# A hybrid decoder step: eight expert steps per block of the second group instead of twelve, and value rows one unit behind the key rows

## Chip, cores and metric

One Trainium2 chip, one core of it. The time is the device time of one execution in microseconds (us). Compared are medians of several executions.

## What is computed

The kernel takes 544 tokens of 2048 channels: a prompt of 512, and 8 samples of 4. They pass a recurrent branch and a convolution branch, which are merged by gates, and then an expert mixer. All parameters are shared. The part that the change touches is the mixer:

```python
q = (xb @ w_q).astype(f32).reshape(PEER_BLOCK, PEER_HEADS, 2, D_HALF)
s1 = jnp.einsum('thd,hkd->thk', q[:, :, 0], keys1.astype(f32))
s2 = jnp.einsum('thd,hkd->thk', q[:, :, 1], keys2.astype(f32))
v1, i1 = lax.top_k(s1, PEER_TOPK)
v2, i2 = lax.top_k(s2, PEER_TOPK)
...
e = (jnp.take_along_axis(i1, si // PEER_TOPK, axis=-1) * N_KEYS
     + jnp.take_along_axis(i2, si % PEER_TOPK, axis=-1))
g = jax.nn.softmax(sv, axis=-1)
u = u_tab[e]
act = jax.nn.gelu(jnp.einsum('thkd,td->thk', u, xb).astype(f32))
v = v_tab[e]
return jnp.einsum('thk,thkd->td', (g * act).astype(xb.dtype), v)
```

Each token has 8 heads, and each head picks 16 of 16384 experts. For each pick a key row of `u_tab` and a value row of `v_tab` (8 KB each) are read.

## The kernel before

Tokens stand in tiles of 128 partitions. A *unit* is one head of one tile, or for the sample tile one of two packed units: there are 34. One *row* of a unit is one pick for 128 tokens: a gather of 1.05 MB by an indirect DMA, issued by POOL. A key row is multiplied with the normalised tokens and summed on VectorE (a dot). A value row is scaled by the pick's weight and added.

The tokens are treated in two groups. Group 0 (the last prompt tile and the samples) goes through branches, w_out and w_q first. It has the first 10 units, 160 rows of either kind. Group 1 (three prompt tiles, 384 columns) follows, with 24 units. While PE multiplies for group 1, VectorE works on the rows of group 0. This is written out by hand in *expert steps*: step p does the dot of key row p (`dot_row`, L1174) and adds value row p - 18 (`value_row`, L1183). There are 178 steps; from step 160 on they hold value rows alone. At row 1 of a unit the weights of the unit before are made (`expert_weights`, L1169), and at row 3 the next unit is routed (`route`, L1131 to L1164: sorting, indices, gates). The functions `steps_branch`, `steps_out` and `steps_query` say which steps stand in which block:

- the branch stage has eight blocks; in each PE makes four products (192 matmul records, 12 weight pieces of 0.5 MB) and VectorE merges two rows of them (`merge`, L1071 to L1075). On VectorE a block holds four steps, the merges of the block before, and eight more steps;
- w_out has sixteen output rows in eight products of 64 records, each with two steps and an addition (`add_rows`, L1098), which waits for a transpose on PE (L1477);
- w_q has eight heads with four steps each. Its scores are copied by ScalarE (`head`). ScalarE follows the same table: the activation of a unit's dots (L827) and the exponents of the next (L822) stand behind the head of that place;
- what is left of the 178 steps comes behind w_q.

POOL issues the gathers in one order, key row p and then value row p - 19, as buffers come free: three for key rows, two for value rows. The weight pieces are loaded by SP into four buffers.

Then come the 24 units of group 1 (line 1236 on). Key rows have four buffers, `u_b`, and value rows four more, `v_b`. POOL issues one of each in turn. The value rows here are added by PE: ScalarE makes a diagonal matrix of the weights (`diagonals`, L843), PE multiplies the row with it into PSUM in four matmuls (L1542, eight records), and VectorE adds the unit's sum (`add_unit`, L1243). `LEAD` is 2: the value rows of unit v are gathered beside the key rows of unit v + 2, so the first two units have key rows alone and the last two value rows alone. POOL's loop copies the indices of a unit into one of two small tiles first (L570). The residual rows come back from DRAM, with the final gain, when w_q is done.

Of the kernel before, what the change touches and what calls it, by code (L numbers as in the profile page):

```python
# [24 lines left out]
I32 = mybir.dt.int32  # L25
# [44 lines left out]
LEAD = 2  # L70
# [63 lines left out]
def hybrid_step(nc, x_prompt, x_sample, state_rnn_conv, state_rnn_h, state_cm_conv, g_mix, w_in,  # L134
# [15 lines left out]
    with ExitStack() as ctx:  # L150
# [151 lines left out]
        idx_v = [cutf(16, I32) for _ in range(2)]  # L302
# [55 lines left out]
        dot_a, v_added, fold_done, fold_read = sem("dot_a"), sem("v_added"), sem("fold_done"), sem("fold_read")  # L358
        staged_scores, top_ready, exp_ready = sem("staged_scores"), sem("top_ready"), sem("exp_ready")
        routed, idx_copied = sem("routed"), sem("idx_copied")  # L360
# [136 lines left out]
        def _(pool):  # L497
# [59 lines left out]
            def u_row(u, parity, k):  # L557
                s = k % SLOTS
                pool.wait_ge(dot_b, u * TOPK + (k + 1))
                gather(u_rows, u_b[s], ub_landed[s], idx_u[parity], k)  # L560

            def v_row(v, parity, k):
                s = k % SLOTS
                pool.wait_ge(v_used, v * TOPK + (k - SLOTS + 1 + TOPK))
                gather(v_rows, v_b[s], vb_landed[s], idx_v[parity], k)

            def v_indices(v, parity):


                nc.gpsimd.tensor_copy(idx_v[parity], idx_all[:, bass.ds(v * TOPK + ROWS_A, TOPK)]).then_inc(idx_copied, 1)  # L570
                pool.wait_ge(idx_copied, v + 1)
# [6 lines left out]
            pool.wait_ge(v_added, ROWS_A)  # L578
            pool.wait_ge(q_done, 2 * HEADS + 2)
            with pool.Fori(0, (UNITS_B - LEAD) // 2) as i:  # L580
                for n in range(2):
                    u = i * 2 + (LEAD + n)
                    pool.wait_ge(routed, u + (UNITS_A + 1))
                    v_indices(i * 2 + n, n)
                    for k in range(TOPK):
                        u_row(u, n, k)
                        v_row(i * 2 + n, n, k)
            for v in range(UNITS_B - LEAD, UNITS_B):
                v_indices(v, v % 2)
# [981 lines left out]
```

## Time and profile before

| | us |
|---|---|
| median of 3 executions | 4137.86 (4135.47 to 4138.53) |
| profiled execution, device time | 4142.44 |
| its span in the trace | 4140.7 |
| PE busy | 3160.5 (76%) |
| VectorE busy | 2436.7 (59%) |
| POOL busy | 1543.4 (37%) |
| ScalarE busy | 557.3 (13%) |
| DMA, mean over the span | 331 GB/s, 1372 MB |

Times in the trace count from the start of its span. Busy shares are means over stages with different limits, so the profile has to be read stage by stage. Of the 1372 MB, the gathers move 1145 MB.

### The profile page before, as it was taken

To read this page: it belongs to the slowest core of one execution; us is meant where nothing else is said; L and a number is where in the kernel's file an instruction comes from. 1 tells how busy PE (TensorE), PEld (TensorE's weight loads), DVE (VectorE), ACT (ScalarE), POOL (GpSimd) and SP (SyncE) were. 2 spreads that over 40 slices of the span, in tenths; PEclk is the share of its full clock that TensorE was granted. 3 is DMA by queue.
4 is the path that set the end of the run, shared out by engine and by line. 5 is a ranking of instruction groups with operands and counts; after the bars stand their busy time and mean duration, and the time that the engine had idled before them with its cause. 6 is when DMAs were issued, how large, how long until landed. Compare 5 with 4: busy or idle time off the path is not lost.

```text
span 4140.7 us, 36271 instructions
## 1 busy us (share of the span) xinstructions
PE 3160.5 (76%) x11848; PEld 1897.9 (46%) x11848; DVE 2436.7 (59%) x3355; ACT 557.3 (13%) x1118; POOL 1543.4 (37%) x1154
## 2 busy tenths in 40 slices
PE   6999899879788866839802777777777777777778
PEld 5999889875445433525500222222222222222233
DVE  2788810146787784775667556655655665566540
ACT  4444310110010000001101001001001100110010
POOL 2000000014454543552335545554454554444432
PEclk9999999889999988979956999999999999999999
DMA  4322367579999998996978999999999999999997
GB/s 124 86 84 84 118 211 242 179 276 335 391 379 389 392 381 312 368 376 224 348 264 346 412 421 421 421 419 422 418 419 418 417 419 416 422 412 422 421 396 253
DMA packets 406310, 1372.28 MB, mean 331 GB/s; under 512 B 24449, under 2 KB 264065, under 8 KB 264735
## 3 DMA queue, kind: packets, MB, share of 16 engines
q0 software_dynamic: 157584, 1145.05, 68.3%
q1 hardware_dynamic: 246382, 221.85, 16.9%
q10 hardware_dynamic: 2257, 4.40, 0.3%
q8 instruction: 33, 0.54, 0.1%
q14 instruction: 54, 0.44, 0.0%
HBM read 1363.20 MB, written 8.86 MB: 331 GB/s over the span
## 4 chain that ended last, share of the span: by engine, by line
DMA 47%; PE 31%; DVE 12%; issue 7%; POOL 2%; ACT 1%; SPq 0%; POOLq 0%; DVEq 0%; ACTq 0%
DMA region<-in_v_tab_dram,region 35%; PE ps L1359 11%; DMA region<-in_u_tab_dram,region 10%; PE ps L1542 8%; DVE region L1183 3%; PE ps L1342 3%; PE ps L1344 3%; PE ps L1343 3%; DVE region L1236 2%; POOL region L523 2%; DVE region L1174 1%; DMA region<-in_state_rnn_h_dram 1%; DMA region<-in_w_q_dram 1%; DVE region L1135 0%; DVE region L1025 0%
## 5 line engine op out<-in xcount | busy, mean ns | idle before, releaser
L1542 PE MATMUL ps<-region,region 128*128 128x512 f32 x3072 | 1418.3, 607 | 579.2 <-DMA region<-in_v_tab_dram,region 572.9
L1359 PE MATMUL ps<-region,region 128*128 128x160 f32 (+1 forms) x5120 | 1241.3, 405 | 182.7 <-DVE region L1071 60.7
L1236 DVE SCALAR_TENSOR_TENSOR region<-region,region 128x2048 f32<-128x2048 f32 x384 | 874.2, 2291 | 624.7 <-DMA region<-in_u_tab_dram,region 624.7
L1542 PEld LDWEIGHTS ps<-region,region 128*128 128x128 f32 x3072 | 561.2, 191 | 1436.4 <-issue 1140.7
L523 POOL DMA_INDIRECT region<-in_v_tab_dram,region x544 | 744.5, 1369 | 1143.5 <-PE ps L1542 554.8
L1359 PEld LDWEIGHTS ps<-region,region 128*128 128x128 f32 x5120 | 863.9, 197 | 552.4 <-issue 114.3
L523 POOL DMA_INDIRECT region<-in_u_tab_dram,region x544 | 756.2, 1390 | 952.9 <-DVE region L1164 340.7
L1183 DVE SCALAR_TENSOR_TENSOR region<-region,region,region 128x2048 f32<-128x2048 f32 x160 | 376.1, 2351 | 245.1 <-DMA region<-in_v_tab_dram,region 245.1
L1174 DVE SCALAR_TENSOR_TENSOR region<-region,region 128x2048 f32<-128x2048 f32 x160 | 365.2, 2285 | 22.3 <-DMA region<-in_u_tab_dram,region 22.3
L1342 PE MATMUL ps<-region,region 128*128 128x272 f32 x1024 | 297.4, 290 | 0.0
L1344 PE MATMUL ps<-region,region 128*128 128x272 f32 x1024 | 296.4, 289 | 0.0
L1343 PE MATMUL ps<-region,region 128*128 128x272 f32 x1024 | 294.8, 288 | 0.0
L827 ACT ACTIVATE region<-region 128x16 f32<-128x16 f32 x34 | 7.3, 216 | 1409.6 <-DVE region L1236 1229.3
L1343 PEld LDWEIGHTS ps<-region,region 128*128 128x128 f32 x1024 | 193.0, 189 | 0.0
L1342 PEld LDWEIGHTS ps<-region,region 128*128 128x128 f32 x1024 | 192.7, 188 | 0.0
L1344 PEld LDWEIGHTS ps<-region,region 128*128 128x128 f32 x1024 | 192.6, 188 | 0.0
L1243 DVE TENSOR_TENSOR region<-region,ps 128x2048 f32<-128x2048 f32 x24 | 54.9, 2288 | 183.3 <-PE ps L1542 183.3
L537 POOL DMA_DIRECT2D region<-in_x_prompt_dram x1 | 0.6, 576 | 388.3 <-DVE region L1080 388.3
L843 ACT ACTIVATE region<-region 128x128 f32<-128x128 f32 x384 | 116.1, 387 | 48.2 <-PE ps L1542 45.5
L822 ACT ACTIVATE region<-region 128x16 f32<-128x16 f32 x34 | 10.5, 307 | 746.2 <-DVE region L1147 746.1
L1025 DVE SCALAR_TENSOR_TENSOR region<-region,region,region 128x512 f32 (+1 forms) x120 | 89.2, 744 | 0.0
L1025 DVE SCALAR_TENSOR_TENSOR region<-region,region 128x512 f32<-128x512 f32 x112 | 83.3, 744 | 0.0
(202 smaller groups left out, 1432.9 us busy)
## 6 DMA issues: line engine op xcount, KB each, us to landing
region<-in_w_in_dram SPq DMA_DIRECT2D x192, 512.0 KB
region<-in_w_out_dram SPq DMA_DIRECT2D x64, 512.0 KB
region<-in_w_q_dram SPq DMA_DIRECT2D x64, 512.0 KB
region<-in_w_a_dram SPq DMA_DIRECT2D x32, 512.0 KB
region<-in_w_b_dram SPq DMA_DIRECT2D x32, 512.0 KB
region<-in_u_tab_dram,region POOLq DMA_INDIRECT x544, 11.6
region<-in_v_tab_dram,region POOLq DMA_INDIRECT x544, 15.3
region<-in_x_prompt_dram SPq DMA_DIRECT2D x7, 1024.0 KB, 15.3
```

Of the source, the lines that this page charges most:

```text
L523: pool.indirect_dma_start(out=slot, out_offset=None, in_=rows_ap, in_offset=bass.IndirectOffsetOnAxis(ap=idx[:, k:k + 1], axis=0)).then_in ...
L843: nc.scalar.activation(diag[:, k, :], ident, ACT.Copy, scale=w_all[:, ROWS_A + v * TOPK + k:ROWS_A + v * TOPK + k + 1]).then_inc(diag_read ...
L1025: mark(stt(out=run, in0=glupad[:, k:k + TP], scalar=tap(k), in1=run, op0=ALU.mult, op1=ALU.add))
L1174: stt(out=u_a[s], in0=u_a[s], scalar=1.0, in1=xn_tile(u), op0=ALU.mult, op1=ALU.mult, accum_out=dots[u % 2][:, p % TOPK:p % TOPK + 1]).the ...
L1183: stt(out=xf[u >> 3], in0=v_a[s], scalar=w_all[:, v:v + 1], in1=xf[u >> 3], op0=ALU.mult, op1=ALU.add).then_inc(v_added, 1)
L1236: stt(out=u_b[s], in0=u_b[s], scalar=1.0, in1=xn_tile(UNITS_A + u), op0=ALU.mult, op1=ALU.mult, accum_out=dots[u % 2][:, k:k + 1]).then_in ...
L1243: tt(tile_v, tile_v, acc[v % 2], ALU.add).then_inc(acc_read, 1)
L1342: mm(halves[j][:, a, :], hi, xh[:, k, h], start=(k == 0), stop=False)
L1343: mm(halves[j][:, a, :], hi, xl[:, k, h], start=False, stop=False)
L1344: last = mm(halves[j][:, a, :], lo, xh[:, k, h], start=False, stop=(k == DC - 1))
L1359: last = mm(outs[n][:, 0:WIDTH[g]], wide[s][:, q, n * P:(n + 1) * P], rhs(k), start=(k == 0), stop=(k == n_k - 1))
L1542: last = mm(acc[n][:, b * 512:(b + 1) * 512], diag[:, k, :], v_b[s][:, b * 512:(b + 1) * 512], start=(k == 0), stop=(k == TOPK - 1))
```

## The change

Two tables of numbers are moved, and with them work between stages. A branch block has 8 steps instead of 12, a pair of output rows 3 instead of 4, and a head of w_q 3 instead of 4. Steps 126 to 177 stand behind w_q, where it was 174 to 177. In the loop over 24 units `LEAD` becomes 1, in the sense that value rows of unit u - 1 go beside key rows of unit u, and the weights of a unit are made behind the second dot of the next. Of the last unit's sixteen value rows VectorE adds five (picks 2, 5, 8, 11, 14) itself, and PE eleven. The index copies on POOL go; POOL's loop is written out.

```diff
-LEAD = 2
+LEAD = 1
+SHARED = tuple(k for k in range(TOPK) if k % 3 == 2)
...
 def steps_branch(m):
-    return 14 + 12 * m, 26 + 12 * m
+    return 14 + 8 * m, 22 + 8 * m
...
 def steps_out(j):
-    return 110 + 2 * j, 112 + 2 * j
+    first = 78 + 3 * (j // 2) + j % 2
+    return first, first + 1 + j % 2
...
 def steps_query(h):
-    return 142 + 4 * h, 146 + 4 * h
+    return 102 + 3 * h, 105 + 3 * h
+
+
+PE_ROWS = (tuple(range(TOPK)), tuple(k for k in range(TOPK) if k not in SHARED))
...
@@ gpsimd
             pool.wait_ge(dot_a, ROWS_A)
-            for u in range(LEAD):
+            pool.wait_ge(routed, UNITS_A + 1)
+            for k in range(TOPK):
+                u_row(0, k)
+            pool.wait_ge(v_added, ROWS_A)
+            pool.wait_ge(q_done, 2 * HEADS + 2)
+            for u in range(1, UNITS_B):
                 pool.wait_ge(routed, UNITS_A + u + 1)
                 for k in range(TOPK):
-                    u_row(u, u, k)
...
+                    u_row(u, k)
+                    v_row(u - 1, k)
+            for k in range(TOPK):
+                v_row(UNITS_B - 1, k)
@@ scalar
             for u in range(UNITS_B):
-                if u >= LEAD:
-                    diagonals(u - LEAD)
                 if u < UNITS_B - 1:
                     stage_scores(UNITS_A + u + 1)
                     exponents(UNITS_A + u + 1)
...
-            diagonals(UNITS_B - 2)
-            diagonals(UNITS_B - 1)
+                diagonals(u)
@@ vector
             for u in range(UNITS_B):
                 for k in range(TOPK):
                     dot(u, k)
+                    if k == 1 and u:
+                        expert_weights(UNITS_A + u - 1)
                     if k == 3 and u < UNITS_B - 1:
                         route(UNITS_A + u + 1)
-                expert_weights(UNITS_A + u)
-                if u >= LEAD:
-                    add_unit(u - LEAD)
+                    if k == 5 and u > LEAD:
+                        add_unit(u - LEAD - 1)
                 if u == TIDY + 1:
                     normalised(slice(0, NT - 1), 4)
-            for v in range(UNITS_B - LEAD, UNITS_B):
-                add_unit(v)
+            last = UNITS_B - 1
+            expert_weights(UNITS_A + last)
+            add_unit(last - 1)
...
+            for n, k in enumerate(SHARED):
+                s, e = k % SLOTS, ROWS_A + last * TOPK + k
+                dve.wait_ge(vb_landed[s], last * (16 * TOPK // SLOTS) + 16 * (k // SLOTS + 1))
...
+                stt(out=xfb[2], in0=v_b[s], scalar=w_all[:, e:e + 1], in1=xfb[2],
+                    op0=ALU.mult, op1=ALU.add).then_inc(end_added, 1)
+            dve.wait_ge(end_added, len(SHARED))
+            add_unit(last)
```

VectorE at the start of w_out, before. L1075 is the last merge, L1174 a dot, L1183 a value row, L1169 the weights of a unit, L1098 an addition of an output row:

```order
L1075 TENSOR_TENSOR region_66<-region_95,region_97 128x384
L1174 SCALAR_TENSOR_TENSOR region_77,region_96<-region_77,region_63 128x2048
L1183 SCALAR_TENSOR_TENSOR region_62<-region_78,region_98,region_62 128x2048
L1174 SCALAR_TENSOR_TENSOR region_75,region_96<-region_75,region_63 128x2048
L1183 SCALAR_TENSOR_TENSOR region_62<-region_79,region_98,region_62 128x2048
L1098 TENSOR_TENSOR region_58<-region_58,ps 128x384
```

The same place in the changed kernel, where these lines are L1070, L1169, L1178, L1164 and L1093:

```order
L1070 TENSOR_TENSOR region_66<-region_95,region_97 128x384
L1169 SCALAR_TENSOR_TENSOR region_75,region_96<-region_75,region_63 128x2048
L1178 SCALAR_TENSOR_TENSOR region_62<-region_78,region_98,region_62 128x2048
L1093 TENSOR_TENSOR region_58<-region_58,ps 128x384
L1169 SCALAR_TENSOR_TENSOR region_76,region_96<-region_76,region_63 128x2048
L1178 SCALAR_TENSOR_TENSOR region_62<-region_79,region_98,region_62 128x2048
L1169 SCALAR_TENSOR_TENSOR region_77,region_96<-region_77,region_63 128x2048
L1178 SCALAR_TENSOR_TENSOR region_62<-region_78,region_98,region_62 128x2048
L1093 TENSOR_TENSOR region_58<-region_58,ps 128x384
```

One step stands ahead of the first addition and two ahead of the second, where it was two and two.

VectorE in the loop of group 1, before, where unit 2 ends. L1236 is a dot, L1169 the weights of the unit, L1243 the addition of the unit two back:

```order
L1236 SCALAR_TENSOR_TENSOR region_82,region_96<-region_82,region_72 128x2048
L1236 SCALAR_TENSOR_TENSOR region_83,region_96<-region_83,region_72 128x2048
L1169 TENSOR_TENSOR region_98<-region_96 128x16
L1243 TENSOR_TENSOR region_88<-region_88,ps 128x2048
L1236 SCALAR_TENSOR_TENSOR region_80,region_96<-region_80,region_72 128x2048
L1236 SCALAR_TENSOR_TENSOR region_81,region_96<-region_81,region_72 128x2048
```

In the changed kernel, where unit 2 begins (L1231 a dot, L1164 the weights, L1238 the addition; the routing stands at the dots):

```order
L1231 SCALAR_TENSOR_TENSOR region_80,region_96<-region_80,region_72 128x2048
L1231 SCALAR_TENSOR_TENSOR region_81,region_96<-region_81,region_72 128x2048
L1164 TENSOR_TENSOR region_98<-region_96 128x16
L1231 SCALAR_TENSOR_TENSOR region_82,region_96<-region_82,region_72 128x2048
L1231 SCALAR_TENSOR_TENSOR region_83,region_96<-region_83,region_72 128x2048
...
L1231 SCALAR_TENSOR_TENSOR region_80,region_96<-region_80,region_72 128x2048
L1231 SCALAR_TENSOR_TENSOR region_81,region_96<-region_81,region_72 128x2048
L1238 TENSOR_TENSOR region_88<-region_88,ps 128x2048
```

The weights of a unit have moved from behind its last dot to behind the second dot of the next unit, and the addition of the unit two back from the end of a unit to behind its sixth dot.

## Rows read from the trace of the kernel before

**Rows 1.** Stages by stretch: engines' busy us, clock, DMA share, rate.

```profile
core 0: us, PE busy (x) PEld busy (x) DVE busy (x) ACT busy (x) POOL busy (x), PEclk, DMA share, GB/s
937.75:1608.36 670.61, 530.25 (x1537) 302.17 (x1537) 509.47 (x565) 43.28 (x75) 325.68 (x193) 0.90 0.98 381
...
1652.50:1855.50 203.00, 137.08 (x429) 80.48 (x427) 161.45 (x182) 11.46 (x24) 112.51 (x59) 0.85 0.95 367
...
1879.70:2064.90 185.20, 179.00 (x608) 108.76 (x608) 105.00 (x99) 18.55 (x39) 61.26 (x39) 0.99 0.80 295
...
2132.60:2245.70 113.10, 0.00 (x0) 0.00 (x0) 91.11 (x142) 7.01 (x16) 66.56 (x34) 0.51 0.76 280
2245.70:4014.30 1768.60, 1304.77 (x2809) 511.14 (x2809) 1050.47 (x1529) 184.33 (x485) 865.96 (x725) 0.99 1.01 419
4014.30:4140.70 126.40, 113.53 (x264) 50.04 (x264) 9.54 (x6) 14.63 (x36) 27.98 (x31) 0.97 0.75 263
```

**Rows 2.** Waits of PE, 1058 to 1606 us: total, times, longest.

```profile
PE ps L1359 <- DVE region L1071: 60.7, 6, 18.2
PE ps L1359 <- DMA region<-in_w_in_dram: 34.7, 18, 4.1
PE ps L1359 <- DMA region<-in_w_a_dram: 5.1, 1, 5.1
```

**Rows 3.** Timeline of PE in w_q and before: start, length, operation.

```profile
1651.95 0.82 PE L1477 MATMUL ps<-region,region 128*128 128x128 f32 x6
...
1922.40 20.81 PE L1359 MATMUL ps<-region,region 128*128 128x384 f32 x64
1943.04 1.50 PE L1486 MATMUL ps<-region,region 128*128 128x128 f32 x12
```

**Rows 4.** Waits of PE, 1606 to 2070 us.

```profile
PE ps L1359 <- DMA region<-in_w_q_dram: 5.2, 3, 3.3
```

**Rows 5.** Timeline of DVE in the branch stage.

```profile
1482.71 2.35 DVE L1183 SCALAR_TENSOR_TENSOR region<-region,region,region 128x2048 f32<-128x2048 f32 x1 [3.05 <-DMA region<-in_v_tab_dram,region]
...
1507.54 2.35 DVE L1183 SCALAR_TENSOR_TENSOR region<-region,region,region 128x2048 f32<-128x2048 f32 x1 [1.50 <-DMA region<-in_v_tab_dram,region]
...
1524.37 0.29 DVE L1131 MAX8 region<-region 128x8 f32<-128x128 f32 x1
...
1535.01 0.23 DVE L1164 TENSOR_SCALAR region<-region 128x16 f32<-128x16 f32 x1
```

**Rows 6.** Timeline of DVE beside w_out.

```profile
1810.98 2.35 DVE L1183 SCALAR_TENSOR_TENSOR region<-region,region,region 128x2048 f32<-128x2048 f32 x1 [0.45 <-DMA region<-in_v_tab_dram,region]
...
1820.54 0.55 DVE L1098 TENSOR_TENSOR region<-region,ps 128x384 f32<-128x384 f32 x1
...
1846.42 2.35 DVE L1183 SCALAR_TENSOR_TENSOR region<-region,region,region 128x2048 f32<-128x2048 f32 x1 [0.91 <-DMA region<-in_v_tab_dram,region]
```

**Rows 7.** Timeline of DVE beside w_q.

```profile
1924.65 0.18 DVE L1169 TENSOR_TENSOR region<-region 128x16 f32<-128x16 f32 x1 [25.06 <-ACT region L827]
...
1968.68 2.35 DVE L1183 SCALAR_TENSOR_TENSOR region<-region,region,region 128x2048 f32<-128x2048 f32 x1 [3.61 <-DMA region<-in_v_tab_dram,region]
...
2032.50 2.35 DVE L1183 SCALAR_TENSOR_TENSOR region<-region,region,region 128x2048 f32<-128x2048 f32 x1 [1.18 <-DMA region<-in_v_tab_dram,region]
```

**Rows 8.** Waits of DVE beside w_q.

```profile
DVE region L1131 <- ACT region L818: 11.7, 1, 11.7
```

**Rows 9.** Timeline of DVE, value rows alone.

```profile
2096.62 2.35 DVE L1183 SCALAR_TENSOR_TENSOR region<-region,region,region 128x2048 f32<-128x2048 f32 x1 [5.65 <-DMA region<-in_v_tab_dram,region]
...
2113.93 2.35 DVE L1183 SCALAR_TENSOR_TENSOR region<-region,region,region 128x2048 f32<-128x2048 f32 x1 [2.93 <-DMA region<-in_v_tab_dram,region]
...
2122.82 2.35 DVE L1183 SCALAR_TENSOR_TENSOR region<-region,region,region 128x2048 f32<-128x2048 f32 x1 [2.98 <-DMA region<-in_v_tab_dram,region]
```

**Rows 10.** Timeline of POOL there.

```profile
2108.38 0.94 POOL L523 DMA_INDIRECT region<-in_v_tab_dram,region  x1 [4.59 <-DVE region L1183]
```

**Rows 11.** Timeline of PE at the end.

```profile
4014.30 113.54 PE L1542 MATMUL ps<-region,region 128*128 128x512 f32 x264 [1.29 <-DMA region<-in_v_tab_dram,region]
```

More of the change, by code:

```diff
@@ L301, in hybrid_step @@
         idx_u = [cutf(16, I32) for _ in range(2)]
-        idx_v = [cutf(16, I32) for _ in range(2)]
         dots = [cutf(16) for _ in range(2)]
@@ L555, in _, with u_row @@
                     gather(v_rows, v_a[v % SLOTS_V], va_landed[v % SLOTS_V], idx_all, v)
-            def u_row(u, parity, k):
-                s = k % SLOTS
+            def u_row(u, k):
+                s, e = k % SLOTS, ROWS_A + u * TOPK + k
                 pool.wait_ge(dot_b, u * TOPK + (k + 1))
[L560 to L565, printed above, removed]
@@ L567, in v_indices, with v_row @@
-            def v_indices(v, parity):
-                nc.gpsimd.tensor_copy(idx_v[parity], idx_all[:, bass.ds(v * TOPK + ROWS_A, TOPK)]).then_inc(idx_copied, 1)
-                pool.wait_ge(idx_copied, v + 1)
-            pool.wait_ge(dot_a, ROWS_A)
-            for u in range(LEAD):
+                gather(u_rows, u_b[s], ub_landed[s], idx_all, e)
+            def v_row(v, k):
+                s, e = k % SLOTS, ROWS_A + v * TOPK + k
+                if v < UNITS_B - 1 or k < SLOTS:
+                    pool.wait_ge(v_used, v * TOPK + (k - SLOTS + 1 + TOPK))
+                else:
+                    shared = sum(1 for n in SHARED if n <= k - SLOTS)
+                    pool.wait_ge(v_used, v * TOPK + (k - SLOTS + 1 - shared + TOPK))
+                    pool.wait_ge(end_added, shared)
+                gather(v_rows, v_b[s], vb_landed[s], idx_all, e)
@@ L580, in _ @@
[L580 to L587, printed above, removed]
-            for v in range(UNITS_B - LEAD, UNITS_B):
-                v_indices(v, v % 2)
-                for k in range(TOPK):
-                    v_row(v, v % 2, k)
+                    u_row(u, k)
@@ L839, in diagonals @@
                 act.wait_ge(w_ready, UNITS_A + v + 2)
-                for k in range(TOPK):
-                    act.wait_ge(v_used, v * TOPK + (k + 1))
+                for n, k in enumerate(PE_ROWS[v == UNITS_B - 1]):
+                    act.wait_ge(v_used, v * TOPK + (n + 1))
                     part(act)
-                    nc.scalar.activation(diag[:, k, :], ident, ACT.Copy,
+                    nc.scalar.activation(diag[:, n, :], ident, ACT.Copy,
                                          scale=w_all[:, ROWS_A + v * TOPK + k:ROWS_A + v * TOPK + k + 1]).then_inc(diag_ready, 1)
@@ L1532, in _, with value_rows @@
             pe.wait_ge(fold_read, 1)
-            with pe.Fori(0, UNITS_B // 2) as i:
-                for n in range(2):
-                    v = i * 2 + n
-                    pe.wait_ge(acc_read, v + 1)
-                    for k in range(TOPK):
-                        s = k % SLOTS
-                        pe.wait_ge(diag_ready, v * TOPK + (k + 1))
-                        pe.wait_ge(vb_landed[s], v * (16 * TOPK // SLOTS) + 16 * (k // SLOTS + 1))
-                        for b in range(4):
-                            last = mm(acc[n][:, b * 512:(b + 1) * 512], diag[:, k, :],
-                                      v_b[s][:, b * 512:(b + 1) * 512], start=(k == 0), stop=(k == TOPK - 1))
-                        last.then_inc(v_used, 1)
+            def value_rows(v, n, rows):
+                pe.wait_ge(acc_read, v + 1)
+                for m, k in enumerate(rows):
+                    s = k % SLOTS
+                    pe.wait_ge(diag_ready, v * TOPK + (m + 1))
+                    pe.wait_ge(vb_landed[s], v * (16 * TOPK // SLOTS) + 16 * (k // SLOTS + 1))
+                    for b in range(4):
+                        last = mm(acc[n][:, b * 512:(b + 1) * 512], diag[:, m, :],
+                                  v_b[s][:, b * 512:(b + 1) * 512], start=(m == 0), stop=(m == len(rows) - 1))
+                    last.then_inc(v_used, 1)
+            with pe.Fori(0, UNITS_B // 2 - 1) as i:
+                for n in range(2):
+                    value_rows(i * 2 + n, n, PE_ROWS[0])
+            value_rows(UNITS_B - 2, 0, PE_ROWS[0])
+            value_rows(UNITS_B - 1, 1, PE_ROWS[1])
 _INS = ['x_prompt', 'x_sample', 'state_rnn_conv', 'state_rnn_h', 'state_cm_conv', 'g_mix', 'w_in',
```

12 lines of the change are left out of this document (7 added, 5 removed).

## The prediction

> **What bounds the kernel now.** I read the table by stretch first, because the change touches every stage from 938 us on and each has another limit [rows 1]. In the second group's branch stage (937.75 to 1608.36) the DMA engines are busy 0.98 of the time, and yet the stage's pace is that of VectorE: a block holds twelve expert steps, and PE waits 60.7 us in six pieces for the merge L1071, which stands behind steps on VectorE, against 39.8 us (34.7 + 5.1) for weights [rows 2]. The same table shows PE idle for a third of the w_out stretch (137.1 of 203.0 us busy), and busy for nearly all of w_q (179.0 of 185.2) [rows 1]. Behind w_q PE has nothing for 67.7 us, until the loop. The loop over 24 units is something else: from 2245.7 to 4014.3 the share is 1.01 at 419 GB/s, so there the gathers themselves are the bound, 1768.6 us for 22 units, 80.4 us each. Its two ends are not: the first two units have key rows alone (113.1 us at 280 GB/s), and the last two have value rows alone (126.4 us at 263 GB/s), where PE works through 264 matmul records in 113.5 us without a gap [rows 1, 11].
>
> **What a step costs.** A step is one key row and one value row. Beside the branch weights the value row of VectorE comes back after 24.8 us for four steps, 6.2 us each; a routing piece adds 10.8 us (1524.4 to 1535.2) [rows 5]. In the quiet end of w_out it is six steps in 35.4 us, 5.9 [rows 6]; over the whole w_out stretch 30 steps, two routings (21.6) and fifteen additions of 0.55 (8.2) fill 203.0 us, which leaves 5.8 [rows 1, 6]. Beside w_q it is ten in 63.8 us, 6.4 [rows 7]. VectorE works only 4.7 us of them (2.3 for the dot, 2.35 for the addition); the rest it waits for the value row, which has two buffers: a new gather starts when a buffer has been added, and must land before the second next addition. Value rows alone take 4.37 us (26.2 us for six) [rows 9].
>
> **Branch stage: 12 steps a block become 8.** VectorE then needs 8 x 6.2 = 49.6, half a routing 5.4, and 3 for the six operations of two merges, taken at the 0.55 us of an addition of the same size [rows 6]: 58 us. PE needs 192 matmul records, and in w_q, at a granted clock of 0.99, 64 take 20.81 us [rows 1, 3]: 62.4 us. So PE takes over as the bound. To that come waits for weights: before they are 39.8 us over eight blocks, 5.0 each; beside w_q they are 5.2 us in 8 x 64 records, which scales to 2.0 for a block [rows 2, 4]. I take 4.0, since fewer gathers compete but PE no longer stands still while its four buffers fill. Eight blocks of 66.4 plus the last merges make 534 to 536 us against 670.6: **135 us saved**. Bounds: no wait (62.4, 167 saved), and twice today's (72.4, 87 saved).
>
> **w_out: 4 steps per pair become 3.** The first addition still comes 44 us after the last merge, since it waits for two products on PE. After it VectorE has 23 steps x 5.8 = 133, two routings 21.6 and additions 8.2: 163 us. PE has seven pairs of 20.81 + 2 x 0.82 + about 0.8 of waiting, 163 too [rows 3]. Two chains of one length that wait for each other in turn don't run at that length; I take 172, **31 us saved** (bounds 40 and 20). w_q now starts 166 us earlier.
>
> **w_q and the rows behind it.** PE's 185.2 us stay. But the exponents and the activation of a unit are on ScalarE in a written order behind its heads. Before, step 145 waited 25.1 us for head 0, and the route of step 147 another 11.7 [rows 7, 8]. Now the stage begins with step 102, and three steps go to a head: the weights of step 113 stand behind head 3, the route of step 115 behind head 4. Head 0 released at 45 us from the start of w_q, and one head takes 20.8 + 1.5 less overlap, 22 us [rows 3, 7], so head 3 releases at 111. VectorE is there after two steps whose rows wait already, 4.7 each, and nine at 6.3 (between 6.2 and 6.4), at 66: it **waits 45 us, longer than now**. It does steps 113 to 115, waits for head 4 and routes until 147, and after ten steps, at 206 us, it stands before step 126. PE has been done for 20 us.
>
> Then come 34 steps with both rows, 18 with value rows alone, and two routings. I price the pair at 5.8, from the stretches with least weight traffic: 197 us. Routings 21.6. The reload of the residual rows and the final gain (4.2 MB, 10 us at 419 GB/s) now falls among these steps, half hidden: 5. Value rows alone: 17 x 4.37 and 9.8 from the last of them (2122.8) to the first key row of the loop (2132.6): 84 [rows 1, 9]. In sum 206 + 197 + 22 + 5 + 84 = 514 us from the start of w_q to the loop, where it was 185.2 + 67.7 = 252.9: **261 us added**. The loop starts 261 - 166 = 95 us later. Bounds of the pair's price: 5.0, which is 2.1 MB at 419 GB/s, and 6.4, as beside w_q: -27 and +20 us.
>
> The rule that speaks for the lower bound: the Trainium skill (DMA: Bandwidth & Descriptors, section Anatomy of one DMA) fits a GpSimd-issued transfer as 2.0 us plus its bytes at 436 GB/s, 4.4 us for such a row. Here the row issued at 2108.38 is used at 2113.93, 5.6 us later, with little else on the queue [rows 9, 10], so the trace says over a microsecond more. By the page a pair would be held by bandwidth alone, and the sum would be 27 us lower.
>
> **The loop, value rows one unit behind.** One unit of key rows alone (56.5) and one of value rows alone go; one paired unit (80.4) comes. Behind the last key row there were 113.5 us of PE work for 33 rows, 3.44 each [rows 11]. Now there are 16 rows and one left over: 17 gathers at 2.5 us are 42.5, the last row's four matmuls 3.4, and 2 for the start; a buffer turns in some 10 us (5.6 to land, 3.4 on PE, 1 to issue), four of them just keep up: 48 us [rows 10, 11]. PE has 11 of the rows, 38 us, and is no longer the limit; VectorE's five at 2.35 lie beside. 113.1 + 113.5 = 226.6 becomes 56.5 + 80.4 + 48 = 185: **42 us saved** (bounds 35 and 48). What hides the later weights: the diagonals of a unit now start some 8 us into the next, but seven gathers of 2.5 us are queued then, so the DMA engines keep working; VectorE is busy 1050 of 1768.6 us there, so its later pieces fit. POOL's index copies and its loop cost nothing either way: it is busy 866 of them [rows 1]. If that cover were gone, each us by which a unit is late costs 23.
>
> **Sum.** The profiled execution took 4142.4 us, 1.7 above its span, and 4.6 above the median of 4137.9. -135 - 31 + 261 - 42 = +53: the execution would take 4195 us, the median **4190**.
>
> **Rivals.**
> - *Late rows at the pace of DMA.* The pair behind w_q takes 5.0 us and the stall in w_q is shorter, because ScalarE is not as late as I count: 4164, and 4141 with half of the stall gone. For it: VectorE has 4.7 us of work in a step. Against it: the value row's wait is there in the quiet stretch too [rows 6].
> - *The loop starves.* The diagonals wait for weights that are a unit younger, PE frees the value buffers late, and POOL, which issues both kinds in one order, holds the key rows behind them. At 3 us a unit, 23 units, 69 us: 4259. The DMA share in the loop would fall from 1.01 below 0.98. It starts once PE's first row of a unit is later than the queued gathers last, 17 us; I count 8.
> - *Faster: a moved row gives back its full price.* The place is the end of a branch block. If VectorE's 58 us stay the bound and PE keeps up, eight blocks save another 8.3 each, 66 us: 4124. It decides from a block of 59.8 us downward. Against it: 192 records at 0.325 us are 62.4, without any wait. For it: records of PE are modelled in part.
> - *Nothing measurable.* The passes and the late rows cancel against the loop, within 8 us of 4138.
>
> **How the numbers follow.** 0.2% is 8 us, about what a measurement of this kernel tells from no change. My forecast, 4155 to 4230 by its own bounds, has 0.62; late rows at DMA pace 0.15; a starving loop 0.10; full price 0.08; nothing 0.05. The first three are slower, but for a little of the second: slower 0.86, same 0.05, faster 0.09. The range 4140 to 4240 leaves out the full price and most of the starving loop.
>
> **What would show it.** In the new profile: branch stage 535 us with PE busy over 0.9 of it and no wait for L1066, the merge's new line; w_out from its first addition 172; a wait of VectorE of some 45 us for ScalarE in w_q; 330 us between the end of w_q on PE and the first key row of the loop; then units of 80.4 us at 419 GB/s, and 48 us of matmuls behind the last key row. I am wrong if the branch stage ends under 500 us or over 590, if steps behind w_q take under 5.2 us, or if the loop's rate falls.

## The result and the profile after

The changed kernel takes 4249.47 us (median of 4 executions, 4240.88 to 4264.53), the kernel before 4138.19 (4 executions, 4135.47 to 4142.28): ratio 1.0272, 95% interval 1.0242 to 1.0302, slower by 111 us. The forecast was 4190. The profiled execution took 4264.53 us at a span of 4262.7, the longest of the four, so the stages below add up to 122 us and not to 111.

The stages of the changed kernel, cut at the same events as before (PE's first record of the stage, its first of w_out, the first and the last addition of w_out, w_q on PE, the first and the seventeenth dot of the loop, its last dot):

```profile
core 0: us, PE busy (x) PEld busy (x) DVE busy (x) ACT busy (x) POOL busy (x), PEclk, DMA share, GB/s
939.30:1508.70 569.40, 517.36 (x1537) 295.87 (x1537) 348.39 (x393) 36.88 (x63) 213.37 (x129) 0.97 0.87 332
1508.70:1553.00 44.30, 44.30 (x133) 26.05 (x134) 2.89 (x4) 2.15 (x3) 3.25 (x2) 0.94 0.46 154
1553.00:1728.00 175.00, 132.11 (x429) 78.03 (x427) 129.91 (x161) 11.56 (x25) 82.03 (x45) 0.90 0.89 341
1728.00:1752.30 24.30, 8.09 (x48) 7.85 (x48) 11.53 (x13) 11.52 (x16) 1.41 (x2) 0.56 0.68 243
1752.30:1944.00 191.70, 181.03 (x608) 109.50 (x608) 97.75 (x98) 17.06 (x37) 68.33 (x39) 0.98 0.73 276
1944.00:2281.10 337.10, 6.55 (x8) 1.24 (x8) 238.29 (x212) 10.67 (x17) 166.32 (x95) 0.51 0.84 313
2281.10:2336.60 55.50, 0.00 (x0) 0.00 (x0) 45.13 (x71) 1.81 (x4) 35.20 (x17) 0.50 0.70 261
2336.60:4194.60 1858.00, 1380.16 (x2934) 555.58 (x2935) 1095.06 (x1599) 196.31 (x511) 903.66 (x734) 0.95 1.01 416
4194.60:4262.70 68.10, 45.54 (x99) 18.53 (x97) 21.25 (x12) 7.12 (x16) 16.84 (x14) 0.92 0.71 266
```

Beside [rows 1] and its last rows, stage by stage:

| stage | before | after | change | forecast |
|---|---|---|---|---|
| branch stage | 670.6 | 569.4 | -101 | -135 |
| w_out from its first addition | 203.0 | 175.0 | -28 | -31 |
| start of w_q to the loop | 252.9 | 528.8 | +276 | +261 |
| loop and its ends | 2008.1 | 1981.6 | -26.5 | -42 |
| rest (start, two gaps) | | | +2 | 0 |
| sum | | | +122 | +53 |

Each term has the forecast's sign, and all four missed upward. In the branch stage PE is now busy 517 of 569 us, VectorE only 348, DMA share 0.87 where it was 0.98. PE took over as the bound, as foreseen, but it waits:

```profile
engine line waited for: us in total, times, longest us
PE ps L1367 <- DMA region<-in_w_in_dram: 32.3, 19, 5.4
PE ps L1367 <- DMA region<-in_w_b_dram: 11.9, 6, 3.0
PE ps L1367 <- DMA region<-in_w_out_dram: 5.2, 1, 5.2
PE ps L1367 <- DVE region L1120: 4.2, 1, 4.2
PE ps L1367 <- DMA region<-in_w_a_dram: 2.5, 2, 1.7
```

That is 51.9 us for weight pieces: 46.7 in the eight blocks, and 5.2 for the first piece of w_out, beside the last merges. The same question asked of the kernel before, over its whole stage (937.75 to 1608.36):

```profile
PE ps L1359 <- DVE region L1071: 60.7, 6, 18.2
PE ps L1359 <- DMA region<-in_w_in_dram: 39.3, 21, 4.1
PE ps L1359 <- DVE region L1075: 35.2, 1, 35.2
PE ps L1359 <- DMA region<-in_w_a_dram: 5.1, 1, 5.1
```

[rows 2] begins at 1058, inside the second block, and so shows 39.8 us for weights where the stage has 44.4. For merges PE waited 95.9 us, with the 35.2 at the stage's end, where w_out's first product waits for the last merge (L1075), and this stands behind eight steps on VectorE. In the changed kernel no wait for a merge is left: the 4.2 us for VectorE (L1120) fall at the start of the stage, ahead of the first block. The 101 us won are these 95.9 and 12.9 of PE's own busy time, less 2.3 more for the branch's weights and the 5.2 for w_out's first piece. The wait for weights did not fall with the gathers, as forecast; it grew a little.

VectorE's waits from the start of w_q to the loop:

```profile
DVE region L1178 <- DMA region<-in_v_tab_dram,region: 114.6, 65, 5.2
DVE region L1164 <- ACT region L825: 55.3, 1, 55.3
DVE region L1126 <- ACT region L816: 11.7, 1, 11.7
```

and the places of its second and third row in VectorE's timeline (start, length, operation, idle time before it):

```profile
1877.56 0.18 DVE L1164 TENSOR_TENSOR region<-region 128x16 f32<-128x16 f32 x1 [55.28 <-ACT region L825]
...
1898.39 0.29 DVE L1126 MAX8 region<-region 128x8 f32<-128x128 f32 x1 [11.68 <-ACT region L816]
```

The stop for ScalarE is 55.3 us, 45 were forecast, and 25.06 stood there before [rows 7]. A stop of 11.7 us before the next routing is there as before [rows 8].

### The profile page after: what moved, and what is told of

Same layout as the page of the kernel before. It is cut to its first block, busy times and chain, and to the rows that moved or that the text cites. A ratio compares the mean times of both kernels' runs of the same rounds, so it can differ in the third digit from the quotient of the medians.

```text
span 4262.7 us, 35344 instructions
## 1 busy us (share of the span) xinstructions
PE 3155.2 (74%) x11808; PEld 1904.6 (45%) x11808; DVE 2448.4 (57%) x3360; ACT 557.2 (13%) x1113; POOL 1549.9 (36%) x1130
## 4 chain that ended last, share of the span: by engine, by line
DMA 39%; PE 38%; DVE 9%; issue 7%; POOL 4%; SPq 1%; ACT 1%; DVEq 0%; POOLq 0%; ACTq 0%
PE ps L1367 21%; DMA region<-in_v_tab_dram,region 20%; DMA region<-in_u_tab_dram,region 11%; PE ps L1548 6%; DMA region<-in_w_in_dram 4%; POOL region L528 4%; PE ps L1350 3%; PE ps L1352 3%; PE ps L1351 3%; DVE region L1178 2%; DVE region L1231 2%; DMA region<-in_w_q_dram 1%; DMA region<-in_w_out_dram 1%; DVE region L1130 1%; DMA region<-in_state_rnn_h_dram 1%
## 5 line engine op out<-in xcount | busy, mean ns | idle before, releaser
L1367 PE MATMUL ps<-region,region 128*128 128x160 f32 (+1 forms) x5120 | 1227.0, 402 | 100.4 <-DMA region<-in_w_in_dram 35.9
L1231 DVE SCALAR_TENSOR_TENSOR region<-region,region 128x2048 f32<-128x2048 f32 x384 | 876.2, 2291 | 739.1 <-DMA region<-in_u_tab_dram,region 738.9
L528 POOL DMA_INDIRECT region<-in_v_tab_dram,region x544 | 756.5, 1391 | 1364.3 <-PE ps L1548 674.7
L1178 DVE SCALAR_TENSOR_TENSOR region<-region,region,region 128x2048 f32<-128x2048 f32 x160 | 376.2, 2351 | 214.0 <-DMA region<-in_v_tab_dram,region 213.9
L1169 DVE SCALAR_TENSOR_TENSOR region<-region,region 128x2048 f32<-128x2048 f32 x160 | 365.3, 2285 | 24.0 <-DMA region<-in_u_tab_dram,region 23.2
L825 ACT ACTIVATE region<-region 128x16 f32<-128x16 f32 x34 | 7.3, 216 | 1504.2 <-DVE region L1231 1244.2
L841 ACT ACTIVATE region<-region 128x128 f32<-128x128 f32 x379 | 113.3, 387 | 219.9 <-DVE region L1164 219.9
L1126 DVE MAX8 region<-region 128x8 f32<-128x128 f32 (+1 forms) x102 | 34.5, 338 | 127.1 <-ACT region L816 120.1
```

The source lines that it names most:

```text
L528: pool.indirect_dma_start(out=slot, out_offset=None, in_=rows_ap, in_offset=bass.IndirectOffsetOnAxis(ap=idx[:, k:k + 1], axis=0)).then_in ...
L841: nc.scalar.activation(diag[:, n, :], ident, ACT.Copy, scale=w_all[:, ROWS_A + v * TOPK + k:ROWS_A + v * TOPK + k + 1]).then_inc(diag_read ...
L1169: stt(out=u_a[s], in0=u_a[s], scalar=1.0, in1=xn_tile(u), op0=ALU.mult, op1=ALU.mult, accum_out=dots[u % 2][:, p % TOPK:p % TOPK + 1]).the ...
L1178: stt(out=xf[u >> 3], in0=v_a[s], scalar=w_all[:, v:v + 1], in1=xf[u >> 3], op0=ALU.mult, op1=ALU.add).then_inc(v_added, 1)
L1231: stt(out=u_b[s], in0=u_b[s], scalar=1.0, in1=xn_tile(UNITS_A + u), op0=ALU.mult, op1=ALU.mult, accum_out=dots[u % 2][:, k:k + 1]).then_in ...
L1367: last = mm(outs[n][:, 0:WIDTH[g]], wide[s][:, q, n * P:(n + 1) * P], rhs(k), start=(k == 0), stop=(k == n_k - 1))
```

## Experiments

Times are medians beside those of the kernel before, which ran on the same chip. Where only one execution is given, the profile is what counts. In "Expected" stands what was written before the run.

**Apart: the tables, and the loop.** The first kernel is the one before with nothing but the three new step tables; the second is the changed kernel with nothing but the old ones.

```diff
 def steps_branch(m):
-    return 14 + 8 * m, 22 + 8 * m
+    return 14 + 12 * m, 26 + 12 * m
...
```

That is one of the three tables (`steps_out` and `steps_query` go back likewise) in e2_loop; e1_tables has the same lines the other way round.

Expected of e1_tables: 

> The kernel before with the three step tables of the changed one, and its own loop over 24 units (value rows two units behind). Theory A, read from the trace of the changed kernel: all of the loss is in the tables, the loop only gives back some 27 us, so this is the slowest of all: 4249 + 27 = about 4275 us (+3.3%), with the first key row of the loop near 2275 us. Theory B, the prediction's sizes: tables +95, so 4233. Theory C, the loop's new form costs time itself: this is faster than 4249.

Expected of e2_loop: 

> The changed kernel with the step tables of before (12, 2 and 4 steps): only the loop over 24 units is new. Theory A: 27 us less than before, 4111 us, with units of 80.9 us. Theory B, the prediction's sizes: 42 less, 4096. Theory C, the loop starves: 4138 or more.

Measured: tables alone 4281.94 beside 4140.38, ratio 1.0351 (1.0331 to 1.0371), +141.6. Loop alone 4111.23 beside the same, 0.9926 (0.9909 to 0.9943), -29.2. The sum, +112.4, is the whole change's +111, so the two parts don't touch each other, and the loop's half is a gain of its own.

**What PE needs with few or no steps beside it.** Branch blocks with no expert steps, and with four; the 64 and 32 steps are not dropped but done later.

```diff
 def steps_branch(m):
-    return 14 + 8 * m, 22 + 8 * m
+    return 14, 14
```

for e3_blocks0, and for e8_blocks4

```diff
 def steps_branch(m):
-    return 14 + 8 * m, 22 + 8 * m
+    return 14 + 4 * m, 18 + 4 * m
```

with `steps_out` and `steps_query` 64 and 32 steps lower. (In e3_blocks0 the four steps ahead of a block's merges are limited to the block's own, so that none is done there.)

Expected of e3_blocks0: 

> The changed kernel with no expert steps in the eight branch blocks at all; the 64 steps come later, behind w_q. Read is the branch stage alone. Theory A: a block of 70.9 us instead of the forecast 66.4 is due to gathers that delay the weight pieces, and to the low clock after such waits; without gathers a block takes 62.4 to 64 and the stage 500 to 515 us, with next to no wait of PE for weights. Rival: the pieces are late by themselves (four buffers, one issuing queue), and the stage stays near 569 us. The whole run should be some 64 x 5.9 - 60 = 320 us longer, about 4570.

Expected of e8_blocks4: 

> The changed kernel with four steps in a branch block instead of eight; 32 more steps behind w_q. With none a block took 61.9 us, with eight 70.9. If each step's gathers delay the weights by the same amount, a block takes 66.4; if the delay comes only when the DMA engines are nearly full (eight steps: 331 GB/s in the stage), it is under 64. The run is some 32 x 5.8 + 11 x 2 - 36 = 170 us longer than the changed kernel.

Measured, the branch stage of either, e3_blocks0 first (whole times 4589.42 and 4399.05, one execution each):

```profile
936.40:1436.70 500.30, 497.46 (x1537) 292.62 (x1537) 29.32 (x53) 13.95 (x32) 4.32 (x3) 1.00 0.37 115
```

```profile
936.30:1445.60 509.30, 499.54 (x1537) 291.91 (x1537) 183.53 (x221) 24.77 (x47) 106.46 (x65) 1.00 0.67 241
```

With four steps PE waits 6.9 us for weight pieces, seven times and never longer than 1.4 us.

With no steps a block takes 61.9 us (the first merges of the eight blocks start at 990.2 to 1423.6), beside the 62.4 that were forecast for 192 records. That is the floor, and PE never waits for a weight. With four steps the stage is 9 us longer, a block 63.3 us on the mean and so under the 64 of the expectation; with eight steps the stage is 69 us longer. The busy column splits the 69: PE's own records grew from 497.5 to 517.4 us, 19.9, and 51.9 are the waits for weights (the no-step kernel waits 2.8 us for a merge where this one does not). The records grow with a granted clock of 0.97 in place of 1.00. Counted from the record starts of the changed kernel, some 80 of its 1537 records take 43 us, where they would take 26 at the length of the others; they stand behind the stops. One such place, in the timeline of the changed kernel:

```profile
1064.51 5.40 PE L1367 MATMUL ps<-region,region 128*128 128x384 f32 x16 [1.41 <-DMA region<-in_w_b_dram]
1072.16 7.12 PE L1367 MATMUL ps<-region,region 128*128 128x384 f32 x16 [2.25 <-DMA region<-in_w_b_dram]
```

Sixteen records behind a wait of 1.41 us take 5.40 us; sixteen behind one of 2.25 take 7.12.

Where the waits fall says more than their sum. Three stretches of the changed kernel's branch stage, the middle one with 33 us in which VectorE waits for ScalarE and so takes no rows:

```profile
984.00:1095.00 111.00, 99.33 (x291) 56.29 (x292) 87.68 (x98) 7.62 (x12) 52.90 (x32) 0.97 0.94 362
1095.00:1170.00 75.00, 75.00 (x234) 44.13 (x233) 35.78 (x54) 3.73 (x8) 19.44 (x12) 1.00 0.69 259
1170.00:1232.00 62.00, 49.76 (x145) 27.48 (x144) 48.03 (x43) 5.81 (x8) 29.37 (x19) 0.97 1.03 405
```

It goes on like this to the stage's end: all 46.7 us of the blocks' waits for weights lie in the four stretches with a DMA share of 0.94 to 1.03, and in the three between (0.61 to 0.70) PE does not wait at all. The stage's 0.87 is the mean of two kinds of time.

**Ten steps, with all other gains in place.** The base is e10_best, the best version (below), with twelve steps in a block; e11_ten takes two from each and does the 16 behind w_q.

```diff
 def steps_branch(m):
-    return 14 + 12 * m, 26 + 12 * m
+    return 14 + 10 * m, 24 + 10 * m
```

`steps_out` and `steps_query` stand 16 steps lower.

Expected of e11_ten: 

> As the fastest kernel with earlier weights, but ten steps in a branch block instead of twelve, and 16 more behind w_q. Theory: VectorE needs 62 + 6.8 + 3 = 72 us for a block, PE 71, so a block falls from 82 to some 74 us and the stage gives back 64 us; 16 steps and their routing behind w_q cost 16 x 5.8 + 11 = 104. So 30 to 40 us slower than the kernel beside it. Rival: with ten steps both engines are filled and the step costs the same in either place: no change.

Measured: 4088.87 beside 4141.18, 0.9881 (0.9863 to 0.9899); e10_best on the same chip has 4068.07. So +21 us, less than expected. The branch stages, each from PE's first record of it to PE's first of w_out, e10_best first:

```profile
930.10:1602.20 672.10, 533.74 (x1537) 303.45 (x1537) 509.59 (x565) 44.66 (x76) 317.64 (x193) 0.91 0.98 380
```

```profile
933.10:1527.20 594.10, 522.13 (x1536) 298.15 (x1536) 434.95 (x484) 39.51 (x69) 268.61 (x163) 0.95 0.97 375
```

In e11_ten the last merge ends at 1517.0 already, but PE waits on for w_out's first piece:

```profile
1527.24 22.83 PE L1375 MATMUL ps<-region,region 128*128 128x384 f32 x64 [18.89 <-DMA region<-in_w_out_dram]
```

This makes a curve of what the branch stage gives back for each step taken out of it:

| steps in a block | stage, us | given back per step |
|---|---|---|
| 12 (e10_best) | 672.1 | |
| 10 (e11_ten) | 594.1 | 78.0 / 16 = 4.9 |
| 8 (the changed kernel) | 569.4 | 24.7 / 16 = 1.5 |
| 4 (e8_blocks4) | 509.3 | 60.1 / 32 = 1.9 |
| 0 (e3_blocks0) | 500.3 | 9.0 / 32 = 0.3 |

The late place costs 5.76 us a step and, with one routing of 10.8 us [rows 5] to sixteen steps, 6.4. No row of the table reaches that. From 12 to 10 each step loses 1.5 us, 25 in sum; the profiled executions are 24 us apart and the medians 21. From 10 to 8 three quarters of a step are lost. Counted to the last merge the first two rows would be 5.5 and 1.1: ten us of what e11_ten gives back go into the wait for w_out's first piece.

**The stop for ScalarE.** The same as the changed kernel, but ScalarE does its two operations for the unit earlier in its written order: the activation of step 112 behind head 1, the exponents of step 115 behind head 2.

```diff
+ACT_QUERY = (102, 105, 113, 116, 117, 118, 120, 123, 126)
...
                 head(1, h)
-                expert_steps(*steps_query(h))
+                expert_steps(ACT_QUERY[h], ACT_QUERY[h + 1])
```

Expected: 

> The changed kernel, where ScalarE does the activation of step 112 behind head 1 of w_q instead of head 3, and the exponents of step 115 behind head 2 instead of head 4; all else is the same. Theory A: the two stops of VectorE in w_q (55.3 and about 24 us) are due to ScalarE's written order, and every us of them is paid behind w_q: the stops shrink to under 20 us and the run is 50 to 60 us faster than the changed kernel, about 4195. Rival: the stops move elsewhere (PE's weights get later as gathers go on, or ScalarE holds PE), and the run stays within 15 us of 4249.

Measured: 4218.76 beside 4140.38, 1.0200 (1.0176 to 1.0225), 31 us less than the changed kernel. The waits of VectorE for ScalarE from w_q to the loop:

```profile
DVE region L1167 <- ACT region L828: 14.9, 2, 11.5
DVE region L1129 <- ACT region L819: 11.7, 1, 11.7
```

The 55.3 us became 14.9, 40 less, and the loop begins at 2239.1 and not 2281.1. By medians it is 31, less than the 50 to 60 expected: 14.9 us of the stop stay, and the routing's 11.7 with them. The stop was on the path, and the step table made it: ScalarE's place for the activation comes from the same table.

**Filling the hole at the start of w_out.** In the kernel with the old tables VectorE is idle for most of the 44 us before its first addition. Here 7 of the 32 w_out steps go ahead of it, and there is one step at the last five rows; nothing is moved out of w_out. ScalarE's activation of step 112 goes earlier too.

```diff
+OUT_CUTS = (110, 117, 119, 121, 123, 125, 127, 129, 131, 133, 135, 137, 138, 139, 140, 141, 142)
...
 def steps_out(j):
-    return 110 + 2 * j, 112 + 2 * j
+    return OUT_CUTS[j], OUT_CUTS[j + 1]
```

Expected: 

> The loop-only kernel (12 steps a block, new loop; 4111 us beside 4140) with seven of the 32 w_out steps put ahead of the first addition of w_out, where VectorE stands idle for 35 us, and one step instead of two at the last five additions; ScalarE makes the activation of step 112 ahead of its first block. Theory: work in a hole costs nothing, so w_out gets 20 to 30 us shorter and the run 4085 us. Rival: the longer chain of VectorE delays the first addition and through it PE, and nothing is left: 4111.

Measured: 4083.00 beside 4140.35, 0.9857 (0.9840 to 0.9874), 28 us under e2_loop. The stretch ahead of the first addition and the one from it to the last:

```profile
1610.30:1658.20 47.90, 44.55 (x135) 25.77 (x136) 40.72 (x61) 3.35 (x8) 21.88 (x13) 0.97 0.94 357
1658.20:1832.00 173.80, 134.38 (x426) 77.42 (x424) 130.43 (x130) 10.04 (x21) 92.16 (x52) 0.92 1.00 389
```

The first is 4 us longer than the 44.1 before, and VectorE works 40.7 us in it; the second is 173.8 where it was 203.0 [rows 1]. Together they win 25 us, where taking a quarter of the steps out won 28, and no step has to be paid for later.

**Two attempts on what is left.** e6_front_act adds to e5_front ScalarE's activation of step 144 ahead of head 0. e7_all adds to that: the first unit's sixteen key rows are gathered and multiplied beside the steps that hold value rows alone.

```diff
             act.wait_ge(x1_out, 16)
+            expert_steps(142, 145)
...
+                if ROWS_A <= p < ROWS_A + TOPK:
+                    u_row(0, p - ROWS_A)
...
+                    if ROWS_A < p <= ROWS_A + TOPK:
+                        dot(0, p - ROWS_A - 1)
```

Expected of e6_front_act: 

> As the run with the w_out hole filled, and besides ScalarE makes the activation of step 144 ahead of head 0 of w_q. VectorE's two stops in w_q (25.1 and 11.7 us before) become one of some 15 us. Theory (a stop of VectorE in w_q is paid in full behind it): 20 us less, 4065. Rival: PE holds, no change to 4085.

Expected of e7_all: 

> As the run before it in this list, and besides the 16 key rows of the first unit of group 1 are gathered and multiplied beside the steps that hold value rows alone, which use some 240 to 280 GB/s. Those steps go from 4.4 to about 5.9 us (+24), the unit of key rows alone (56 us) goes but for its routing of 10.8: 20 to 30 us less, 4040. Rival: the two rings in one queue slow each other down to the sum of both, no gain.

Measured: e6_front_act 4083.29 beside 4140.35, 0.9853 (0.9835 to 0.9871), no gain over e5_front. The waits of VectorE from the end of w_out on, e5_front first, then e6_front_act:

```profile
DVE region L1168 <- ACT region L827: 25.2, 1, 25.2
DVE region L1130 <- ACT region L818: 11.7, 1, 11.7
```

```profile
DVE region L1132 <- ACT region L818: 38.1, 1, 38.1
```

Two stops of 25.2 and 11.7 us became one of 38.1. What releases it is ScalarE's staging (L818) of head 0's scores for the routing of step 147. In ScalarE's timeline of e6_front_act L806 copies a head's scores, head 0's in the first line, head 1's in the second:

```profile
1899.80 0.49 ACT L806 ACTIVATE region<-ps 128x384 f32<-128x384 f32 x1 [0.18 <-PE ps L1500]
...
1921.78 0.49 ACT L806 ACTIVATE region<-ps 128x384 f32<-128x384 f32 x1 [0.18 <-PE ps L1500]
1922.17 0.41 ACT L818 ACTIVATE region<-region 128x256 f32<-128x256 f32 x1
```

Head 0's scores are there at 1900.3, and the staging comes at 1922.2, because step 147 belongs to head 1 in the table. So of the 38.1 us some 16 are PE's, which VectorE has to wait for in any order, and some 22 are ScalarE's written order once more. No run puts the staging behind head 0, so what these 22 us are worth is not shown; e7_all has the same stop (38.3 us), and e10_best too (38.4).

e7_all 4069.40 beside the same 4140.35, 0.9829 (0.9809 to 0.9849), 14 us less where 20 to 30 were expected. From the first step with a value row alone to the start of the second unit, e6_front_act first:

```profile
2013.90:2163.30 149.40, 35.32 (x121) 19.70 (x119) 89.79 (x90) 7.96 (x16) 56.94 (x37) 0.62 0.79 281
```

```profile
2006.70:2139.20 132.50, 38.23 (x125) 21.02 (x123) 89.04 (x90) 7.96 (x16) 56.81 (x34) 0.65 0.80 304
```

149.4 us at 281 GB/s became 132.5 at 304: the rows move together, but the rate stays well under the loop's 416 to 419.

**The weights of a unit, early again.** The loop keeps its lag of one unit, but a unit's weights are made right behind its last dot, as before the change. e9_weights does so on e2_loop, e10_best on e7_all.

```diff
                     dot(u, k)
-                    if k == 1 and u:
-                        expert_weights(UNITS_A + u - 1)
...
+                expert_weights(UNITS_A + u)
```

Expected of e9_weights: 

> The loop-only kernel (4111 us beside 4140) with the weights of a unit made right behind its last dot, as before the change, and not behind the second dot of the next. Theory: the late weights stop PE some 7 us at a unit's start (wait for L841), which in part of the units drains the queue, and costs some 10 us over the loop: 4101. Rival: those holes come from routing on VectorE, and nothing changes: 4111.

Expected of e10_best: 

> The fastest kernel so far (4069 us: 12 steps a block, filled w_out hole, the first unit's key rows beside the value rows alone) with the same earlier weights: 4060 by the theory, 4069 by the rival.

Measured: e9_weights 4098.97 beside 4141.18, 0.9901 (0.9884 to 0.9917), against 0.9926 (0.9909 to 0.9943) for e2_loop; the intervals overlap. What PE waits for in the loop, and its stretch, e2_loop first, then e9_weights:

```profile
PE ps L1547 <- DMA region<-in_v_tab_dram,region: 299.5, 232, 2.6
PE ps L1547 <- ACT region L840: 151.6, 22, 10.4
```

```profile
2265.80:4038.20 1772.40, 1320.76 (x2809) 531.90 (x2809) 1049.21 (x1529) 187.93 (x488) 864.09 (x699) 0.95 1.01 418
```

```profile
PE ps L1545 <- DMA region<-in_v_tab_dram,region: 454.0, 339, 4.5
PE ps L1545 <- ACT region L840: 6.3, 1, 6.3
```

```profile
2262.90:4028.10 1765.20, 1304.92 (x2810) 511.35 (x2809) 1050.26 (x1528) 185.74 (x482) 846.32 (x699) 0.99 1.01 419
```

The stop of 6.9 us at each unit (151.6 in 22) is gone, and the stretch is 7 us shorter. PE waits as long as before, only for something else: its wait for value rows grew from 299.5 to 454.0 us, while the gathers keep the DMA engines at a share of 1.01 in both. e10_best has 4068.07 beside 4141.18, 0.9826 (0.9809 to 0.9842), against 0.9829 for e7_all: no difference that can be told. So taking 150 us of PE's waiting for ScalarE away is worth between 0 and 12 us. e10_best is the best version here, 73 us under the kernel before: it has the loop's lag of one unit, and none of the moves between stages.

## Why the prediction came out as it did

**Right in direction and in where the time goes.** Slower, by moving steps from a place where they cost less than their new one. PE took over the branch stage from VectorE; w_out gave back 28 us (31 forecast); the late step with both rows takes 5.76 us (the value rows of steps 126 and 160 start at 1977.2 and 2194.6; less 21.6 for the two routings among them, that is 195.8 us for 34 steps), forecast 5.8; value rows alone took 4.4 us (seventeen from 2194.61 to 2269.77), forecast 4.37. The first rival, late rows at the pace of DMA, is out by this: it wanted 5.0 for the pair, and the DMA share from the end of w_q to the loop is 0.84. The Trainium skill (DMA: Bandwidth & Descriptors, Anatomy of one DMA) fits such a transfer as 2.0 us plus its bytes at 436 GB/s, for this row an estimated 4.4 us; the trace does not agree, with 5.6 us from issue to use [rows 9, 10].

**The step that failed: the branch block of 66.4 us, "62.4 us" for 192 records and "I take 4.0" for the weights.** The eight blocks took 70.5 us each (939.2 to 1503.4). This term costs 34 of the 69 us missed, in two parts.

The larger part, 19.9 us or 2.5 a block, had no term at all: PE's own time was priced at the clock of w_q, 0.99. With no steps beside it that price is right (61.9 measured), but with the gathers beside it the same records are busy 517.4 us at a granted clock of 0.97. The row for it was on the page: in [rows 1] they are busy 530.3 us at 0.90, 66.3 a block.

The smaller part is the waits for weights: 46.7 us in the blocks, 5.8 each, where 4.0 were taken, so 15 us. The forecast's "over eight blocks, 5.0 each" was a misreading, since [rows 2] starts inside the second block; the whole stage had 44.4 us, 5.6 each. And "fewer gathers compete" did not help: a third of the gathers went and the waits grew to 46.7. The 5.2 us of w_q that I scaled down to a block come from a DMA share of 0.80 [rows 1]; here the waits lie in stretches at 0.94 to 1.03. That PE's stops for the merge had let the weight buffers fill, which I had named, fits with this, and no run isolates it.

**The stall in w_q, right in kind, 10 us short in size.** The stop forecast at 45 us was 55.3, and step 126 stood at 220 us and not at 206. VectorE reached the place at 69.9 us (forecast 66), and head 3 released it at 125 (forecast 111). What failed is "one head takes ... 22 us": head 1 took 32, because PE waited there for pieces of w_q's weights, and started again at a lower clock:

```profile
1798.03 1.50 PE L1494 MATMUL ps<-region,region 128*128 128x128 f32 x12
1801.15 5.40 PE L1367 MATMUL ps<-region,region 128*128 128x384 f32 x16 [1.62 <-DMA region<-in_w_q_dram]
1807.79 5.43 PE L1367 MATMUL ps<-region,region 128*128 128x384 f32 x16 [1.24 <-DMA region<-in_w_q_dram]
1816.61 7.12 PE L1367 MATMUL ps<-region,region 128*128 128x384 f32 x16 [3.39 <-DMA region<-in_w_q_dram]
```

L1494 are the scores of head 0. The kernel before had its 5.2 us of such waits further back in w_q, between 2000 and 2023, behind the heads that VectorE waited for. So the routing was over at 157 us (forecast 147), and the ten steps behind it took 63 us and not 59: that is the 14 us, nearly all of the 15 by which this term is short. e4_actq shows that the stop was on the path: 40 us less of it moved the loop 42 us forward in the profile, and 31 by medians.

**The loop, 15.5 us short.** Of "56.5 + 80.4 + 48 = 185" the first held (55.5). Counted from the dots' starts, the units with both rows take 80.98 us where they took 80.7, and the last unit's dots 76.4 where they took 71.0, so that the way from the first to the last dot grew by 34.4 us and not by 24. From the last dot to the end it is 68.1 us, forecast some 63: the last matmul ends at 4249.8, 53 behind the dot's end. The sentence that failed is "the DMA engines keep working" behind later weights. A place in the changed kernel's loop, timeline of PE:

```profile
2657.41 3.67 PE L1548 MATMUL ps<-region,region 128*128 128x512 f32 x8 [1.30 <-DMA region<-in_v_tab_dram,region]
2667.79 18.88 PE L1548 MATMUL ps<-region,region 128*128 128x512 f32 x40 [6.71 <-ACT region L841]
```

PE stands 6.71 us at a unit's start, because the diagonals (L841) wait for the weights, and these for two more dots; ScalarE's first diagonal is at 2667.26, 7.5 us behind the next unit's first dot (2659.77), so the forecast's 8 was right, and yet it is 10 us behind the activation of the unit's last dots (2657.14). The queued gathers cover most of that: of the starving loop's 69 us hardly a tenth came, but not none. With the weights early, e9_weights gained 42 us over the kernel before; with them late it was 29. That 42 is also the forecast's figure is chance, for the forecast had the weights late. That the difference is the waits alone is not settled, since e10_best over e7_all shows next to none.

**The other rivals.** "A moved row gives back its full price" needed a block under 59.8 us; the floor is 61.9, and it is out. "Nothing measurable" is out by the interval.

**Not foreseen.** VectorE waits for ScalarE's staging of the scores in the branch stage too:

```profile
DVE region L1126 <- ACT region L816: 107.8, 4, 33.9
```

107.8 us in four pieces, where the kernel before had one of 8.1: the staging for a routing stands behind the gates of its block on ScalarE, and these wait for PE. No merge came too late for PE by it, which waited for VectorE only 4.2 us, before the first block. But it makes the work uneven: the merges come alternately some 51 and 91 us apart, and the gathers in bursts, in which all of PE's waits for weights lie. Whether steps spread evenly would make these waits shorter is the open question of this case; no run has ScalarE's part earlier in the branch blocks.

## What to carry to other kernels

Moving work from one stage to another is worth what it costs in the old place less what it costs in the new one, and both must be read at the margin. Once another engine is the bound of the old place, the rest of what you take out gives little back (4.9 us a step for the first 16 here, 1.5 for the next 16, against 6.4 in the new place). Filling a hole of the same stage (e5_front) won as much as moving a quarter of its work away, and cost nothing later. When a schedule table sets the order of several engines, look where each engine's part of a moved step lands: the 55 us stop was one small activation queued behind four heads, and the 38 us left in the best version are in good part one staging queued behind a head too many. Price an engine at the clock that it had in that very stage. And a wait counts only by what it holds up: taking away 150 us of PE's waiting for ScalarE in the loop was worth 12 at most.

## What the runs showed of the hardware

The wait of PE for its 96 weight pieces grows out of proportion with the busy share of the DMA engines: 0 us at a share of 0.37, 6.9 at 0.67, 46.7 at 0.87, and within the last all of it in stretches at 0.94 to 1.03, none at 0.61 to 0.70. Stops of a few us cost more than their length: with them the granted clock of the stage was 0.97 and not 1.00, and PE's busy time for the same 1537 records 517.4 us and not 497.5. In e2_loop, with a stop of 6.9 us in each unit, the granted clock is 0.95, in e9_weights without it 0.99, and the busy time 1320.8 and 1304.9.
